# All eight depthwise chunks on VectorE instead of seven beside one on GpSimd, with value and gate products in turn

## The chip, the core and the metric

The kernel runs on one core of a Trainium2 chip. The metric is the device time of one execution in microseconds, here the median of three runs. Lower is better.

## The reference

The kernel computes one step of a diffusion trunk of two layers, for 512 latent tokens and 128 context tokens of 1024 features, all float32. The first layer mixes tokens by a Conformer convolution, the second by a bidirectional Mamba-2 scan; each is followed by an expert-choice mixture of 16 experts. This case is about the convolution of the first layer:

```
def conformer_conv(h, pw1_w, pw1_b, dw_w, dw_b, ln_g, ln_b, pw2_w, pw2_b, axis):
    u = h @ pw1_w + pw1_b
    a, g = jnp.split(u, 2, axis=-1)
    u = a * jax.nn.sigmoid(g)
    ...
    v = depthwise_conv2d(grid, dw_w, dw_b, kh, kw).reshape(bsz, L, dm)
    v = jax.nn.silu(layer_norm(v, ln_g, ln_b))
    return v @ pw2_w + pw2_b
```

The pointwise product makes 2048 features of 1024. Its first half is the value, its second the gate. The depthwise convolution has 31 taps; the latent tokens are a grid of rows of 64, the context tokens one line of 128. Around it stand the modulation vectors, six per layer, from SiLU(cond) @ ada_w[i] + ada_b[i].

## The kernel before, in words

Five engines run programs written out by hand, tied by semaphores. Features lie on the 128 partitions, so the 1024 features are eight chunks (0 to 7), and a chunk holds 640 tokens.

SP only loads weights: units of 2 MB, in the order in which TensorE uses them, into a ring of three slots (`load`, L366 in it). Before a unit goes into a slot it waits until the unit three places earlier has been used; `used` says on which semaphore. Units 0 to 11 are the modulation of layer 0, 12 to 15 the pointwise product (value of chunks 0 to 3, gate of 0 to 3, value of 4 to 7, gate of 4 to 7), 16 to 27 the modulation of layer 1, 28 and 29 the second pointwise product.

TensorE makes the modulation of layer 0 and the transposed input, then the 16 chunk products of the pointwise layer (L469, L470; 512 and 128 tokens), two in flight. It makes them in the order of the units: value of chunks 0 to 3, gate of 0 to 3, and then the same for 4 to 7. Then comes the modulation of layer 1 (L407, L398), and only then the mean over the features of the convolved chunks (L480, L481: a product with a matrix of 1/1024), one chunk after the other in a fixed order, each as soon as its chunk is convolved, and the mean of the squares (L485, L486). Then the second pointwise product.

ScalarE empties the banks. Of a value chunk it writes three pieces into the padded rows `upad` (L917, L919, L921); of a gate chunk it writes sigmoids into `sig` (L924, L926). Each such chunk raises `glu_a` by one.

VectorE and GpSimd share the convolution. `glu` (L313, L315, L318) multiplies value and sigmoid in place. Then a chunk has one product (L1324) and 30 multiply-adds, called taps here (L1328, SCALAR_TENSOR_TENSOR on 128 x 640), into the chunk of `v`. VectorE takes seven chunks in the groups (0), (1, 2), (4, 5), (6, 7):

```
step.sync(len(chunks) - 1 - (j if k == TAPS - 1 else 0))
ins = V.scalar_tensor_tensor(out, rows(k), dw_w[:, c, k:k + 1], out, ALU.mult, ALU.add)
```

`sync(n)` waits until all steps but the last n are complete. In a pair the taps of its two chunks stand in turn and each waits for the last but one; in the lone chunk 0 each waits for the one before. GpSimd takes chunk 3: a product into a buffer (L1162) and an addition (L1164) for each tap. When all eight chunks and their mean are there, VectorE centres them (L1338, L1340), ScalarE squares, TensorE sums, and VectorE goes on to the reciprocal and the scaling (L1342 to L1349).

Of the kernel before, what the change touches and what calls it, by code (L numbers as in the profile page):

```python
# [19 lines left out]
ALU = mybir.AluOpType  # L20
# [3 lines left out]
P = 128  # L24
# [31 lines left out]

CONV_DVE = ((0,), (1, 2), (4, 5), (6, 7))
CONV_ORDER = [c for cs in CONV_DVE for c in cs]
CONV_POOL = (3,)

# [54 lines left out]
def build(nc, w_stream, x_in, params, consts, router, w_dt, ln_rows, pw2_b, ssd_rows, state_in, y_out, state_out):  # L115
    ctx = ExitStack()
    with ctx:
# [56 lines left out]
        sig = take("conv", KC, TOK)  # L174
        pconv = take("conv", 2, TOK)
        sq = take("conv", 2, TOK)
# [88 lines left out]
        def par_v(name, *shape):  # L265
# [13 lines left out]
        landed = [sem(f"slot_landed{i}") for i in range(R)]  # L279
        names = """wo_high wo_low yT_low lgT_ready logits_tr pool_step glu_sig_pool conv_pool x_loaded par_loaded cst_loaded wr_loaded ln_loaded pwb_loaded ssdp_loaded state_loaded  # L280
            dve_step act_step adab_ready cond_ready ada_mm mrow_ready ada_tr mT_ready
# [27 lines left out]
        def glu(c, eng, step, gated, n_gated):  # L309

            i = (c // 4) * 8 + 4 + c % 4
            step.eng.wait_ge(s["glu_a"], i + 1)
            step(eng.tensor_tensor(upad[:, c, 0:8, HALO:HALO + GRID_W], upad[:, c, 0:8, HALO:HALO + GRID_W],  # L313
                                   sig[:, c, 0:SAMPLE].rearrange("p (r w) -> p r w", w=GRID_W), ALU.mult))
            step(eng.tensor_tensor(upad[:, c, 8, HALO:PITCH], upad[:, c, 8, HALO:PITCH],  # L315
                                   sig[:, c, SAMPLE:SAMPLE + PITCH - HALO], ALU.mult))
            step.sync()
            eng.tensor_tensor(upad[:, c, 9, 0:PITCH - HALO], upad[:, c, 9, 0:PITCH - HALO],  # L318
                              sig[:, c, SAMPLE + GRID_W - HALO:TOK], ALU.mult).then_inc(gated, 1)
            step.eng.wait_ge(gated, n_gated)  # L320
# [7 lines left out]
        def _(sp):  # L328
# [7 lines left out]
            def used(u):  # L336
# [3 lines left out]
                if u < U_ADA1:  # L340
                    return s["pw1_done"], 4 * (u - U_PW1 + 1)
                if u < U_PW2:
# [44 lines left out]
        def _(pe):  # L387
# [74 lines left out]
            for i in range(16):  # L462
                if i % 4 == 0:
                    w = unit_wait(U_PW1, i // 4)
                if i >= 2:
                    pe.wait_ge(s["glu_a"], i - 1)
                for k in range(KC):
                    lw = w[:, k, (i % 4) * P:(i % 4 + 1) * P]
                    pe.matmul(bank[i % 2][:, :], lw, hT[:, k, 0:SAMPLE], start=(k == 0), stop=(k == KC - 1))  # L469
                    ins = pe.matmul(bank[2 + i % 2][:, 0:P], lw, hT[:, k, SAMPLE:TOK], start=(k == 0), stop=(k == KC - 1))  # L470
# [3 lines left out]
            pe.wait_ge(s["glu_a"], 16)  # L474
            for i, k in enumerate(CONV_ORDER[:5] + list(CONV_POOL) + CONV_ORDER[5:]):
                if k in CONV_ORDER:
                    pe.wait_ge(s["conv_ready"], CONV_ORDER.index(k) + 1)
                else:
                    pe.wait_ge(s["conv_pool"], CONV_POOL.index(k) + 1)
                pe.matmul(bank[0][:, :], mean_w, v[:, k, 0:SAMPLE], start=(i == 0), stop=(i == KC - 1))  # L480
                ins = pe.matmul(bank[2][:, 0:P], mean_w, v[:, k, SAMPLE:TOK], start=(i == 0), stop=(i == KC - 1))  # L481
            ins.then_inc(s["mean_mm"], 1)
# [372 lines left out]
        def _(act):  # L855
# [55 lines left out]
            for i in range(16):  # L911
                c = (i // 8) * 4 + i % 4
                act.wait_ge(s["pw1_done"], i + 1)
                a, b = bank[i % 2], bank[2 + i % 2]
                if (i // 4) % 2 == 0:
                    bias = pw1_b[:, c:c + 1]
# [223 lines left out]
        def _(pool):  # L1140
# [14 lines left out]
            pool_step = Steps(pool, s["pool_step"])  # L1155
            for c in CONV_POOL:
                glu(c, nc.gpsimd, pool_step, s["glu_sig_pool"], CONV_POOL.index(c) + 1)
                out, rows = taps(c)
                pool_step(nc.gpsimd.tensor_scalar(out, rows(0), dw_w[:, c, 0:1], dw_b[:, c:c + 1], ALU.mult, ALU.add))
                for k in range(1, TAPS):  # L1160
                    prod = pconv[:, k % 2, :].rearrange("p (r w) -> p r w", w=GRID_W)
                    pool_step(nc.gpsimd.tensor_scalar(prod, rows(k), dw_w[:, c, k:k + 1], None, ALU.mult))  # L1162
                    pool_step.sync()
                    ins = nc.gpsimd.tensor_tensor(out, out, prod, ALU.add)  # L1164
                    if k < TAPS - 1:
                        pool_step(ins)
                    else:
                        ins.then_inc(s["conv_pool"], 1)

            def ln_shift(b):  # L1170
# [86 lines left out]
        def _(dve):  # L1257
# [58 lines left out]

            for chunks in CONV_DVE:
                for c in chunks:
                    glu(c, V, step, s["glu_sig"], CONV_ORDER.index(c) + 1)
                for k in range(TAPS):  # L1320
# [12 lines left out]

            dve.wait_ge(s["conv_ready"], len(CONV_ORDER))
            dve.wait_ge(s["conv_pool"], len(CONV_POOL))
            dve.wait_ge(s["mean_mm"], 1)
# [471 lines left out]
```

## Time and profile before

| | before |
|---|---|
| median of three runs | 3122.15 us (3120.74 to 3125.72) |
| profiled execution | its span, 3126.8 us, is the one time on record for it |
| TensorE busy | 2657.5 us, 85% of the span |
| VectorE busy | 2156.3 us, 69% |
| ScalarE busy | 1293.1 us, 41% |
| GpSimd busy | 736.0 us, 24% |

The shares are over the whole span; this case turns on the stretch from about 100 to 425 us. Matmuls of float32 appear as two records each. The times of the section with rows count from the start of the span. GpSimd's durations are rough.

### The profile page before, as it was taken

Reading aid. Unit: us, or ns where it says so; the run is one execution under the profiler, and the core shown is the slowest. Engines: PE = TensorE matmul, PEld = TensorE weight load, DVE = VectorE, ACT = ScalarE, POOL = GpSimd, SP = SyncE. Lnnn points to the kernel's source line nnn. Section 1 sums busy time; section 2 is a strip of 40 time slices with the busy share of each in tenths; the row PEclk is TensorE's granted clock in tenths of the full one; section 3 lists DMA queues with packets and bytes.
Section 4 is the critical chain, followed back from the end, with each engine's and each line's share of the span. In section 5 each row is a group of like instructions: output and inputs, shape, how many; then the busy total and the mean of one; then the engine's idle time right before and its main releaser. Section 6 shows DMA issues by size and latency. Waiting matters only on the chain. (4 is left out here: it accounts for less than half of the span.)

```text
span 3126.8 us, 31580 instructions
## 1 busy us (share of the span) xinstructions
PE 2657.5 (85%) x11808; PEld 1683.5 (54%) x11808; DVE 2156.3 (69%) x2454; ACT 1293.1 (41%) x1573; POOL 736.0 (24%) x345
## 2 busy tenths in 40 slices
PE   8999377888989888939989899898578889988892
PEld 1452133566656666526756556565356665666661
DVE  0099934777786777774656747567777778777777
ACT  1211022556566565622212212122255657656562
POOL 1069002121221212230422304133312121121213
PEclk9999788899999999968999999999789999999996
DMA  8316201566676666721011010110146667666770
GB/s 354 135 54 241 108 3 65 197 257 244 243 296 241 256 244 252 282 73 36 12 68 41 34 69 6 68 54 34 41 182 253 243 263 292 237 250 242 266 269 34
DMA packets 37578, 511.06 MB, mean 163 GB/s; under 512 B 4336, under 2 KB 4352, under 8 KB 6384
## 3 DMA queue, kind: packets, MB, share of 16 engines
q1 hardware_dynamic: 35424, 500.96, 42.8%
q0 software_dynamic: 2064, 8.87, 0.8%
q8 instruction: 60, 0.98, 0.1%
q14 instruction: 30, 0.25, 0.0%
HBM read 505.10 MB, written 4.72 MB: 163 GB/s over the span
## 5 line engine op out<-in xcount | busy, mean ns | idle before, releaser
L970 ACT ACTIVATE w_h<-ring 128x2048 fp32r<-128x2048 f32 x384 | 731.4, 1914 | 277.5 <-PE bank L564 266.9
L1407 DVE TENSOR_TENSOR w_l<-ring,w_h 128x2048 fp32r<-128x2048 f32 x320 | 736.9, 2320 | 132.0 <-ACT w_h L970 131.6
L1148 POOL TENSOR_TENSOR w_l<-ring,w_h 128x2048 fp32r<-128x2048 f32 x64 | 291.8, 4581 | 1331.9 <-ACT w_h L970 1331.9
L562 PE MATMUL bank<-w_h,xin_h 128*80 128x512 f32 x1024 | 409.6, 400 | 35.5 <-DVE w_l L1407 25.8
L563 PE MATMUL bank<-w_l,xin_h 128*80 128x512 f32 x1024 | 403.2, 394 | 0.0
L564 PE MATMUL bank<-w_h,xin_l 128*80 128x512 f32 x1024 | 401.2, 392 | 0.0
L562 PEld LDWEIGHTS bank<-w_h,xin_h 128*80 128x80 f32 x1024 | 151.8, 148 | 144.9 <-DVE w_l L1407 60.3
L1328 DVE SCALAR_TENSOR_TENSOR scr<-scr,par 128x640 f32<-128x640 f32 x210 | 221.4, 1120 | 1.1
L562 PE MATMUL bank<-w_h,hidT_h 128*80 128x512 f32 x512 | 204.7, 400 | 10.1 <-DVE hidT_l L1399 9.1
L563 PE MATMUL bank<-w_l,hidT_h 128*80 128x512 f32 x512 | 202.5, 396 | 0.0
L564 PE MATMUL bank<-w_h,hidT_l 128*80 128x512 f32 x512 | 201.0, 393 | 0.0
L671 PE MATMUL bank<-hT,ring 128*128 128x512 f32 x384 | 198.9, 600 | 2.3 <-DVE scr L1722 2.3
L564 PEld LDWEIGHTS bank<-w_h,xin_l 128*80 128x80 f32 x1024 | 152.1, 149 | 85.3 <-issue 0.9
L563 PEld LDWEIGHTS bank<-w_l,xin_h 128*80 128x80 f32 x1024 | 152.0, 148 | 73.4 <-issue 0.7
L407 PE MATMUL bank<-ring,csil 128*2 128x512 f32 x384 | 169.8, 596 | 10.8 <-DMA ring<-w_stream 10.8
L1226 POOL TENSOR_TENSOR scr<-cst,scr 128x512 f32<-128x512 f32 x80 | 97.9, 1248 | 335.5 <-ACT scr L1075 271.0
L515 PE MATMUL bank<-scr,X 128*128 128x128 f32 x1024 | 152.5, 323 | 0.0
L1398 DVE CAST hidT_h<-bank 128x320 fp32r<-128x320 f32 x64 | 31.1, 485 | 174.0 <-PE bank L570 174.0
L515 PEld LDWEIGHTS bank<-scr,X 128*128 128x128 f32 x1024 | 150.5, 239 | 0.0
L692 PE MATMUL bank<-ring,hT 128*128 128x512 f32 x320 | 149.7, 594 | 0.0
L508 PE MATMUL bank<-scr,X 128*128 128x32 f32 x256 | 57.9, 402 | 101.4 <-DVE scr L1381 101.4
L469 PE MATMUL bank<-hT,ring 128*128 128x512 f32 x256 | 131.0, 594 | 0.0
(260 smaller groups left out, 4286.5 us busy)
## 6 DMA issues: line engine op xcount, KB each, us to landing
ring<-w_stream SPq DMA_DIRECT2D x234, 2048.0 KB, 7.8
ln_gb<-ln_rows POOLq DMA_DIRECT2D x4, 1024.0 KB, 5.1
ring<-w_stream SPq DMA_DIRECT2D x4, 1024.0 KB, 5.0
X<-x_in SPq DMA_DIRECT2D x1, 2560.0 KB, 25.7
y_out<-X SPq DMA_DIRECT2D x5, 512.0 KB, 2.6
scr<-state_in POOLq DMA_DIRECT2D x8, 256.0 KB, 7.3
state_out<-scr POOLq DMA_DIRECT2D x8, 256.0 KB, 5.0
cst<-consts SPq DMA_DIRECT2D x1, 480.0 KB, 11.5
```

The costliest lines, as they stand in the source:

```text
L407: ins = pe.matmul(bank[4 + u % 2][0:2, :], csil[:, k, :], w[:, k, :], start=(k == 0), stop=(k == KC - 1))
L469: pe.matmul(bank[i % 2][:, :], lw, hT[:, k, 0:SAMPLE], start=(k == 0), stop=(k == KC - 1))
L515: ins = pe.matmul(bank[6 + half][:, kk * P:(kk + 1) * P], X[:, t, k * P:(k + 1) * P], psel[:, t, :, :], start=(t == 0), stop=(t == NS - 1))
L562: pe.matmul(out[0:SLOTS, :], ah[:, c, :], wh[:, k, :], start=(c == 0), stop=False)
L563: pe.matmul(out[0:SLOTS, :], ah[:, c, :], wl[:, k, :], start=False, stop=False)
L564: ins = pe.matmul(out[0:SLOTS, :], al[:, c, :], wh[:, k, :], start=False, stop=(c == KC - 1))
L671: pe.matmul(bank[i % 2][:, :], w[:, k, c0:c0 + P], hT[:, k, 0:SAMPLE], start=(k == 0), stop=(k == KC - 1))
L692: ins = pe.matmul(bank[(0, 6, 7, 0, 1)[t]][:, :], hT[:, k, t * P:(t + 1) * P], w[:, k, :], start=(k == 0), stop=(k == KC - 1))
L970: A(w_h[m % NB][:, :, :], src, ACT.Copy).then_inc(s["high_ready"], 1)
L1148: nc.gpsimd.tensor_tensor(w_l[m % NB][:, :, :], src, w_h[m % NB][:, :, :].bitcast(F32), ALU.subtract).then_inc(s["low_pool"], 1)
L1328: ins = V.scalar_tensor_tensor(out, rows(k), dw_w[:, c, k:k + 1], out, ALU.mult, ALU.add)
L1407: V.tensor_tensor(w_l[m % NB][:, :, :], src, w_h[m % NB][:, :, :].bitcast(F32), ALU.subtract)\
```

## The change

Four things are changed.

- GpSimd convolves nothing; chunk 3 goes to VectorE, whose groups are now (0), (1), (2, 3), (4, 5), (6, 7).
- TensorE makes value and gate of a chunk in turn, so chunk 0 has both after two products. ScalarE empties them in that order. The order of the weight units is as before, so that two units are in use at a time, and SP waits for other counts: `(7, 8, 15, 16)` chunk products instead of `(4, 8, 12, 16)`.
- The lone chunks 0 and 1 are summed in two halves, taps 0 to 15 into `v` and taps 16 to 30 into `pconv`, which stand in turn; one addition joins them.
- TensorE takes the means in the order of the chunks.

```
-CONV_DVE = ((0,), (1, 2), (4, 5), (6, 7))
-CONV_ORDER = [c for cs in CONV_DVE for c in cs]
-CONV_POOL = (3,)
+CONV_GROUPS = ((0,), (1,), (2, 3), (4, 5), (6, 7))
+SPLIT_TAP = 16
...
-            i = (c // 4) * 8 + 4 + c % 4
-            step.eng.wait_ge(s["glu_a"], i + 1)
+            step.eng.wait_ge(s["glu_a"], 2 * c + 2)
...
-                    return s["pw1_done"], 4 * (u - U_PW1 + 1)
+                    return s["pw1_done"], (7, 8, 15, 16)[u - U_PW1]
...
             for i in range(16):
-                if i % 4 == 0:
-                    w = unit_wait(U_PW1, i // 4)
+                c, half = i // 2, i % 2
+                w = unit_wait(U_PW1, 2 * (c // 4) + half)
                 if i >= 2:
                     pe.wait_ge(s["glu_a"], i - 1)
                 for k in range(KC):
-                    lw = w[:, k, (i % 4) * P:(i % 4 + 1) * P]
+                    lw = w[:, k, (c % 4) * P:(c % 4 + 1) * P]
...
-            for i, k in enumerate(CONV_ORDER[:5] + list(CONV_POOL) + CONV_ORDER[5:]):
-                if k in CONV_ORDER:
-                    pe.wait_ge(s["conv_ready"], CONV_ORDER.index(k) + 1)
-                else:
-                    pe.wait_ge(s["conv_pool"], CONV_POOL.index(k) + 1)
...
+            for k in range(KC):
+                pe.wait_ge(s["conv_ready"], k + 1)
...
-                c = (i // 8) * 4 + i % 4
+                c = i // 2
...
-                if (i // 4) % 2 == 0:
+                if i % 2 == 0:
...
-            for c in CONV_POOL:
-                glu(c, nc.gpsimd, pool_step, s["glu_sig_pool"], CONV_POOL.index(c) + 1)
-                out, rows = taps(c)
-                pool_step(nc.gpsimd.tensor_scalar(out, rows(0), dw_w[:, c, 0:1], dw_b[:, c:c + 1], ALU.mult, ALU.add))
-                for k in range(1, TAPS):
-                    prod = pconv[:, k % 2, :].rearrange("p (r w) -> p r w", w=GRID_W)
-                    pool_step(nc.gpsimd.tensor_scalar(prod, rows(k), dw_w[:, c, k:k + 1], None, ALU.mult))
-                    pool_step.sync()
-                    ins = nc.gpsimd.tensor_tensor(out, out, prod, ALU.add)
...
+            def conv_alone(c):
+
+                glu(c, V, step, s["glu_sig"], c + 1)
+                out, rows = taps(c)
+                half = pconv.rearrange("p (r w) -> p r w", w=GRID_W)
+                step(V.tensor_scalar(out, rows(0), dw_w[:, c, 0:1], dw_b[:, c:c + 1], ALU.mult, ALU.add))
+                step(V.tensor_scalar(half, rows(SPLIT_TAP), dw_w[:, c, SPLIT_TAP:SPLIT_TAP + 1], None, ALU.mult))
+                for k in range(1, SPLIT_TAP):
+                    step.sync(1)
+                    step(V.scalar_tensor_tensor(out, rows(k), dw_w[:, c, k:k + 1], out, ALU.mult, ALU.add))
+                    if SPLIT_TAP + k < TAPS:
+                        step.sync(1)
+                        step(V.scalar_tensor_tensor(half, rows(SPLIT_TAP + k), dw_w[:, c, SPLIT_TAP + k:SPLIT_TAP + k + 1],
+                                                    half, ALU.mult, ALU.add))
+                step.sync()
+                V.tensor_tensor(out, out, half, ALU.add).then_inc(s["conv_ready"], 1)
+                dve.wait_ge(s["conv_ready"], c + 1)
```

How the order of instructions moves can be seen at two places. The first is ScalarE where it begins to empty the pointwise product; `upad` and `sig` are both parts of the scratch tile `scr`. Before, the fourth value chunk is followed by the first sigmoid:

```order
L917 ACTIVATE scr<-bank,par 128x8x64 [waits pw1_done]
L919 ACTIVATE scr<-bank,par 128x79
L921 ACTIVATE scr<-bank,par 128x79 [waits act_step]
L924 ACT_TABLE_LOAD
L924 ACTIVATE scr<-bank,par 128x512 [waits pw1_done]
```

Of the change, where the lines have moved up by five, from the first value chunk on:

```order
L912 ACTIVATE scr<-bank,par 128x8x64 [waits pw1_done,upad_zero]
L914 ACTIVATE scr<-bank,par 128x79
L916 ACTIVATE scr<-bank,par 128x79 [waits act_step]
L919 ACT_TABLE_LOAD
L919 ACTIVATE scr<-bank,par 128x512 [waits pw1_done]
L921 ACTIVATE scr<-bank,par 128x128 [waits act_step]
L912 ACTIVATE scr<-bank,par 128x8x64 [waits pw1_done]
```

The first sigmoid stood behind four value chunks and now stands behind one. The other sigmoids and value chunks follow in turn.

The second place is VectorE at chunk 0, from its gating to the gating of the next chunk. Before:

```order
L313 TENSOR_TENSOR scr<-scr 128x8x64 [waits glu_a]
L315 TENSOR_TENSOR scr<-scr 128x79
L318 TENSOR_TENSOR scr<-scr 128x79 [waits dve_step]
L1324 TENSOR_SCALAR scr<-scr,par 128x640 [waits glu_sig]
L1328 SCALAR_TENSOR_TENSOR scr<-scr,par 128x640 [waits dve_step] x30
```

Of the change, whose L1325 adds to `v` and L1328 to `pconv`; between the pieces the two stand in turn, 29 in all:

```order
L1321 TENSOR_SCALAR scr<-scr,par 128x640 [waits glu_sig]
L1322 TENSOR_SCALAR scr<-scr,par 128x640
L1325 SCALAR_TENSOR_TENSOR scr<-scr,par 128x640 [waits dve_step]
L1328 SCALAR_TENSOR_TENSOR scr<-scr,par 128x640 [waits dve_step]
...
L1325 SCALAR_TENSOR_TENSOR scr<-scr,par 128x640 [waits dve_step]
L1331 TENSOR_TENSOR scr<-scr 128x640 [waits dve_step]
L311 TENSOR_TENSOR scr<-scr 128x8x64 [waits glu_a,conv_ready]
```

Thirty taps behind each other have become 29 in two chains, with a second product ahead and a sum behind.

## Rows read from the trace of the kernel before

**Rows 1.** The first line of the page

```profile
span 3126.8 us, 31580 instructions
```

**Rows 2.** Busy time of each engine by stretch, granted clock and DMAs

```profile
core 0: us, PE busy (x) PEld busy (x) DVE busy (x) ACT busy (x) POOL busy (x), PEclk, DMA share, GB/s
...
181.00:311.00 130.00, 130.00 (x418) 51.07 (x417) 129.61 (x103) 17.90 (x56) 127.31 (x64) 1.00 0.46 170
311.00:337.00 26.00, 25.57 (x75) 6.06 (x74) 26.00 (x32) 5.04 (x23) 0.82 (x1) 1.00 0.79 283
337.00:393.00 56.00, 7.04 (x25) 3.97 (x24) 55.70 (x75) 0.32 (x3) 0.00 (x0) 0.59 0.08 34
393.00:412.00 19.00, 16.07 (x40) 8.14 (x38) 8.27 (x19) 7.18 (x9) 0.00 (x0) 0.68 0.00 0
```

**Rows 3.** Timeline of VectorE, the convolution: start, us, line, operation, count

```profile
154.63 0.69 DVE L313 TENSOR_TENSOR scr<-scr 128x512 f32<-128x512 f32 x1 [47.55 <-ACT scr L926]
...
156.44 28.39 DVE L1328 SCALAR_TENSOR_TENSOR scr<-scr,par 128x640 f32<-128x640 f32 x30
...
190.24 84.38 DVE L1328 SCALAR_TENSOR_TENSOR scr<-scr,par 128x640 f32<-128x640 f32 x60
...
341.87 0.68 DVE L313 TENSOR_TENSOR scr<-scr 128x512 f32<-128x512 f32 x1
...
344.33 1.14 DVE L1324 TENSOR_SCALAR scr<-scr,par 128x640 f32<-128x640 f32 x2
345.38 47.83 DVE L1328 SCALAR_TENSOR_TENSOR scr<-scr,par 128x640 f32<-128x640 f32 x60
```

**Rows 4.** Taps (L1328) alone in two stretches: us, VectorE busy (count), clock, DMA

```profile
159.20:175.77 16.57, 15.93 (x18) 1.00 0.00 0
...
312.00:341.00 29.00, 29.00 (x37) 1.00 0.78 284
```

**Rows 5.** Timeline of GpSimd, one tap of chunk 3 to the next

```profile
252.84 2.46 POOL L1162 TENSOR_SCALAR scr<-scr,par 128x640 f32<-128x640 f32 x1
...
257.06 2.45 POOL L1162 TENSOR_SCALAR scr<-scr,par 128x640 f32<-128x640 f32 x1
```

**Rows 6.** Timeline of ScalarE, the second, fifth and eighth product emptied

```profile
127.55 0.69 ACT L917 ACTIVATE scr<-bank,par 128x512 f32<-128x512 f32 x1 [7.33 <-PE bank L470]
...
153.51 0.69 ACT L924 ACTIVATE scr<-bank,par 128x512 f32<-128x512 f32 x1 [6.08 <-PE bank L470]
...
179.47 0.69 ACT L924 ACTIVATE scr<-bank,par 128x512 f32<-128x512 f32 x1 [7.57 <-PE bank L470]
```

**Rows 7.** Timeline of TensorE, the means of the chunks

```profile
336.49 1.12 PE L480 MATMUL bank<-scr,cst 128*128 128x512 f32 x2
...
337.67 1.02 PE L480 MATMUL bank<-scr,cst 128*128 128x512 f32 x2
...
338.75 1.02 PE L480 MATMUL bank<-scr,cst 128*128 128x512 f32 x2
...
392.47 2.07 PE L480 MATMUL bank<-scr,cst 128*128 128x512 f32 x2 [47.76 <-DVE scr L1328]
```

**Rows 8.** Timeline of VectorE, centring, after the variance, and scaling

```profile
397.24 0.69 DVE L1338 TENSOR_TENSOR scr<-scr,bank 128x512 f32<-128x512 f32 x1 [4.03 <-PE bank L481]
...
411.08 0.69 DVE L1342 TENSOR_SCALAR scr<-bank 128x512 f32<-128x512 f32 x1 [6.39 <-PE bank L486]
...
416.97 5.97 DVE L1349 TENSOR_TENSOR scr<-scr 128x640 f32<-128x640 f32 x8 [0.80 <-ACT scr L934]
```

**Rows 9.** Timeline of TensorE, the means of the squares

```profile
399.07 2.07 PE L485 MATMUL bank<-scr,cst 128*128 128x512 f32 x2 [1.97 <-ACT scr L932]
...
405.33 1.02 PE L485 MATMUL bank<-scr,cst 128*128 128x512 f32 x2
...
409.80 1.02 PE L485 MATMUL bank<-scr,cst 128*128 128x512 f32 x2
```

**Rows 10.** DMA issues of the page: count, KB each, us from issue to landing

```profile
ring<-w_stream SPq DMA_DIRECT2D x234, 2048.0 KB, 7.8
```

More of the change, by code:

```diff
@@ L174, in build @@
         sig = take("conv", KC, TOK)
-        pconv = take("conv", 2, TOK)
+        pconv = take("conv", TOK)
         sq = take("conv", 2, TOK)
@@ L279, in build @@
         landed = [sem(f"slot_landed{i}") for i in range(R)]
-        names = """wo_high wo_low yT_low lgT_ready logits_tr pool_step glu_sig_pool conv_pool x_loaded par_loaded cst_loaded wr_loaded ln_loaded pwb_loaded ssdp_loaded state_loaded
+        names = """wo_high wo_low yT_low lgT_ready logits_tr pool_step x_loaded par_loaded cst_loaded wr_loaded ln_loaded pwb_loaded ssdp_loaded state_loaded
             dve_step act_step adab_ready cond_ready ada_mm mrow_ready ada_tr mT_ready
@@ L474, in _ @@
             pe.wait_ge(s["glu_a"], 16)
-            for i, k in enumerate(CONV_ORDER[:5] + list(CONV_POOL) + CONV_ORDER[5:]):
-                if k in CONV_ORDER:
-                    pe.wait_ge(s["conv_ready"], CONV_ORDER.index(k) + 1)
-                else:
-                    pe.wait_ge(s["conv_pool"], CONV_POOL.index(k) + 1)
-                pe.matmul(bank[0][:, :], mean_w, v[:, k, 0:SAMPLE], start=(i == 0), stop=(i == KC - 1))
-                ins = pe.matmul(bank[2][:, 0:P], mean_w, v[:, k, SAMPLE:TOK], start=(i == 0), stop=(i == KC - 1))
+            for k in range(KC):
+                pe.wait_ge(s["conv_ready"], k + 1)
+                pe.matmul(bank[0][:, :], mean_w, v[:, k, 0:SAMPLE], start=(k == 0), stop=(k == KC - 1))
+                ins = pe.matmul(bank[2][:, 0:P], mean_w, v[:, k, SAMPLE:TOK], start=(k == 0), stop=(k == KC - 1))
             ins.then_inc(s["mean_mm"], 1)
@@ L1155, in _ @@
             pool_step = Steps(pool, s["pool_step"])
-            for c in CONV_POOL:
-                glu(c, nc.gpsimd, pool_step, s["glu_sig_pool"], CONV_POOL.index(c) + 1)
-                out, rows = taps(c)
-                pool_step(nc.gpsimd.tensor_scalar(out, rows(0), dw_w[:, c, 0:1], dw_b[:, c:c + 1], ALU.mult, ALU.add))
-                for k in range(1, TAPS):
-                    prod = pconv[:, k % 2, :].rearrange("p (r w) -> p r w", w=GRID_W)
-                    pool_step(nc.gpsimd.tensor_scalar(prod, rows(k), dw_w[:, c, k:k + 1], None, ALU.mult))
-                    pool_step.sync()
-                    ins = nc.gpsimd.tensor_tensor(out, out, prod, ALU.add)
[L1165 to L1168, printed above, removed]
             def ln_shift(b):
@@ L1315, in _, with conv_group @@
             hT_evac(0)
-            for chunks in CONV_DVE:
+            def conv_group(chunks):
                 for c in chunks:
-                    glu(c, V, step, s["glu_sig"], CONV_ORDER.index(c) + 1)
+                    glu(c, V, step, s["glu_sig"], c + 1)
                 for k in range(TAPS):
@@ L1332, in _ @@
                             ins.then_inc(s["conv_ready"], 1)
-            dve.wait_ge(s["conv_ready"], len(CONV_ORDER))
-            dve.wait_ge(s["conv_pool"], len(CONV_POOL))
+            def conv_alone(c):
+                glu(c, V, step, s["glu_sig"], c + 1)
+                out, rows = taps(c)
[12 more added lines that the diff above has]
+                dve.wait_ge(s["conv_ready"], c + 1)
+            for chunks in CONV_GROUPS:
+                if len(chunks) == 1:
+                    conv_alone(chunks[0])
+                else:
+                    conv_group(chunks)
+            dve.wait_ge(s["conv_ready"], KC)
             dve.wait_ge(s["mean_mm"], 1)
```

## The prediction

> **What bounds the kernel now.** The execution spans 3126.8 us [rows 1]; the median of the runs shown is 3122.15, so the span lies 4.65 above it. The sum below is a difference between instants of this one execution, and it is taken off the median.
>
> I read the page's 40 slices first: the fifth (312 to 391 us) is where TensorE is emptiest while VectorE is full. The table by stretches [rows 2] makes that sharp. From 181 to 311 us TensorE, VectorE and GpSimd are all full. From 337 to 393 TensorE works 7.04 of 56 us, VectorE 55.70 and GpSimd nothing: TensorE waits 47.76 us for the last taps, and they end it at 392.47 [rows 7]. So the end of this stage is set by VectorE's chain of taps, which starts at 154.63 us, having waited 47.55 us for ScalarE's first sigmoid, and ends at 345.38 + 47.83 = 393.21 [rows 3].
>
> Two things in that chain are to be seen. First its start: ScalarE empties the product of the pointwise layer chunk by chunk, 8.65 us apart, and the sigmoid that starts at 153.51 is the fifth of the 16 [rows 6]. Second its pace. The sixty taps of chunks 1 and 2 take 84.38 us (1.406 each), those of chunks 6 and 7 take 47.83 (0.797 each) [rows 3]. The fast ones ran with GpSimd silent, the slow ones beside it; GpSimd makes one tap in 257.06 - 252.84 = 4.22 us [rows 5], and three slow VectorE taps are 4.22 us too. From 312 to 341 us, after GpSimd's last tap, 37 taps fit in 29 us (0.784), while the DMAs and TensorE run as hard as in the slow stretch [rows 2, 4]. That singles out GpSimd.
>
> **The change, part by part.**
>
> *GpSimd's chunk goes.* Chunk 3 moves to VectorE. No GpSimd work lies beside the taps any more, so I price every interleaved tap at 0.797. Later GpSimd work is not touched. Nothing waited on GpSimd here: its last tap was done by about 312 us, 80 before VectorE's.
>
> *Value and gate in turn.* TensorE's 16 chunk products have the same size and total, and ScalarE's evacuations only change order. The first gate is now the second product instead of the fifth: ScalarE gets it at 127.55, where it now empties a value chunk after 7.33 us of idling [rows 6], and VectorE may start 3 x 8.65 = 25.96 us sooner, at 154.63 - 25.96 = 128.67. The table load that now falls before this sigmoid comes in that idle time of ScalarE and costs nothing; in the old order too there is one only. The gate of chunk 1 is there 17.3 us later, at 146.0, and that of chunk 3 at about 180.6 (it is the eighth product before and after: ScalarE starts on it at 179.47 and takes 1.1 [rows 6]).
>
> *SP's queue.* Unit 15 of the weights (gates of chunks 4 to 7) waits for unit 12's slot, which is free after the seventh product instead of the fourth: 153.51 + 2 x 8.65 = 170.8 us, counted from the fifth. A transfer lands 7.8 us after issue [rows 10], so at 178.6; the tenth product begins when the ninth is out, at 188.1. Unit 17 now waits for the 15th product instead of the 12th (240.0 us), lands at 247.8 and is the second of the modulation's units, wanted some 7 us after that starts at about 248.6. The slack is 9 and 8 us; if it were gone, each us late would be TensorE's. Units 16 and 18 are freed as before.
>
> *Lone chunks in two half sums.* Chunks 0 and 1 each cost: gating and first product 156.44 - 154.63 = 1.81; one more product 1.14/2 = 0.57; 29 alternating taps; the final sum, which waits for everything: a 640-wide TENSOR_TENSOR is 0.75 [rows 8], and 0.25 for the two semaphore turns is an estimate from the 0.125 by which a lone tap's spacing exceeds an interleaved one's. The 29 taps are the term with two candidates. In the old lone chunk, where every tap waits for the one before, 18 taps take 16.57 us, 0.921 each [rows 4]; interleaved ones take 0.797 [rows 3]. The new order lets each tap wait for the last but one, as the pairs do, so I take 0.797: 23.1 us, and 26.5 for the chunk. The upper bound is 0.921: 3.6 us more a chunk, 7.2 in all. Lower bound 0.784: 0.4 less.
>
> The Trainium skill ("VectorE: DVE Perf Modes", section "The DRAIN you can't avoid") says that a semaphore between chained VectorE instructions costs nothing, since the pipeline empties anyway. By it the half sums would buy nothing and the lone chunk would take 0.921 a tap either way, with an extra product and sum on top; the rows at 0.921 and 0.797 speak against it.
>
> *Sum for VectorE.* 128.67 + 2 x 26.5 = 181.7, when chunk 3's gate is there. A pair without GpSimd takes 393.21 - 341.87 = 51.34 [rows 3]; three take 154.0. The taps end at **335.7 us**, against 393.21.
>
> *What is late next.* TensorE. It ends the second modulation at 336.5 and goes straight on to the means [rows 7]. The eight chunks' means now stand behind each other: the spacing is 338.75 - 337.67 = 1.08, the eighth starts at 337.67 + 6 x 1.08 = 344.15 and VectorE can have it 1.28 later, as behind the last variance matmul of the same two shapes (409.80 to 411.08 [rows 8, 9]). VectorE begins to centre at **345.4** instead of 397.24 [rows 8]: **51.8 us** gained. VectorE has slack: chunk 6 is wanted at 344.15 - 1.08 = 343.1, 7.4 after my end of the taps. So even at 0.921 a tap in the lone chunks (342.9) the sum hardly moves.
>
> *The clock.* From 337 to 393 the granted clock averages 0.59, from 393 to 412 0.68 [rows 2]: after its wait TensorE works at the lower of its levels (1.2 GHz) until about 404. The first three variance chunks now take (405.33 - 399.07)/3 = 2.09 us each, the late ones (409.80 - 405.33)/4 = 1.12 [rows 9]. In the new order TensorE arrives from full work at 2.4 GHz and idles about 2 us only. First variance matmul 1.83 us after centring begins, as now; eight at 1.12, the last 1.28: 1.83 + 7 x 1.12 + 1.28 = 10.95, against 411.08 - 397.24 = 13.84 [rows 8]. Gain **2.9 us**. Bounds: 0 if the clock falls in the short pause; for more than 2.9 no row speaks.
>
> Behind 411.08 the same work stands in the same order, each step waiting for the one before, and the ring of three weight slots is filled by TensorE's own progress, so nothing can be done ahead or given back there. Sum: 51.8 + 2.9 = 54.7; 3122.15 - 54.7 is about **3067.5 us** (-1.75%).
>
> **Rivals.**
>
> A. *Taps end after TensorE wants them* (chance 0.10). If lone taps take 0.921 or more, or paired taps beside ScalarE's evacuations over 0.83, chunk 6 is late and every further us is lost, and TensorE may drop a clock level once more. At 0.85 for all 238 taps VectorE ends at 348.3, 5.2 later than wanted, and with the clock's 2.9 lost the time is 3075.6. Against it: 29 us at 0.784 with both other engines at work [rows 4].
>
> B. *It is not GpSimd that slows the taps* (0.03), but some other companion of that stretch, ending at about 312 by chance. Then chunk 3 is simply added to a slow VectorE. Break-even: the 238 taps plus 17.3 us of other work must fit in 393.21 - 128.67 = 264.5, so they may take 1.04 each; above that it is **slower**. At 1.406 for all, the taps take 334.6, and the end comes 87 us later than now: 3209. What speaks for it: GpSimd's stretch is also that of the pointwise product [rows 2]. Against: chunk 4 and 5's own taps turn fast the moment GpSimd stops, under the same transfers at 283 GB/s [rows 2, 4].
>
> C. *The Trainium skill's lock* (0.02 as a result of its own). As a mechanism here: if in each 4.22 us GpSimd kept VectorE out only for part, and VectorE's spacing alone were still above 0.797 for other reasons, removing GpSimd would give less. Halfway, 1.1 a tap, VectorE would end at 408 and the kernel take 3137. The skill ("SBUF — State Buffer", section "Who interferes with whom") has it as an exclusive lock on a shared port pair, the loser waiting for a whole instruction. By that rule the removal frees all of it; the fast rows agree, but three VectorE taps for each pair of GpSimd instructions, which is busy 127.31 of 130 us [rows 2], are more than a strict reading would allow.
>
> D. *The early order does not arrive* (0.03): a weight unit late, or TensorE waiting for ScalarE in the mixed order, shifts the end of the modulation. A landing twice the usual 7.8 us would still be inside unit 15's slack; I price this at up to 6 us lost, 3073.
>
> **How the numbers follow.** Forecast, with TensorE the bound at 345.4: chance 0.82. Its own range is 3063 to 3073: the clock term between 0 and 2.9, half a us each in the start of the means and in the landing of the last one, and 3 us for the spread of medians (the three runs shown lie 5 apart). To hold 8 in 10 with room for A and D I give 3060 to 3076. A measurement of this kernel tells about 0.2% (6 us) from no change. Faster by more than that: forecast, A, D: 0.95. Slower by more: B and part of C, 0.04. Within: 0.01.
>
> **What would show it.** VectorE's first gating near 128.7 us and its last tap near 335.7; the spacing of taps 0.80 from first to last, the lone chunks' as well, about 26.5 us for each of those; no wait of TensorE for taps at all, the eight means behind each other from 336.5; centring from 345.4, variance done by about 356.4, TensorE's clock full until then; everything later moved by 54 to 55 us and of equal length. Wrong it is if the taps keep 1.0 or more, if TensorE idles before the sixth or seventh mean, or if the pointwise product ends later than 248.6.

## The result and the profile after

| | before | after |
|---|---|---|
| median (range, runs) | 3121.44 us (3119.01 to 3125.72, 4) | 3072.82 us (3066.08 to 3075.05, 4) |
| ratio, 95% interval | | 0.983, 0.9814 to 0.9847 |
| profiled execution: time, span | span 3126.8 us | 3066.08, 3064.2 us |
| VectorE's last tap ends | 393.21 us | 334.58 us |
| centring starts | 397.24 us | 345.61 us |
| first residual after the second product | 435.16 us | 380.17 us |

The kernel is 1.7% faster: the medians differ by 48.6 us. The interval of the ratio stands for a gain of 48 to 58 us, and the forecast of 54.7 lies in it. The profiled execution happens to be the fastest of the four.

The stretches of [rows 2], of the changed kernel, with the same columns:

```profile
core 0: us, PE busy (x) PEld busy (x) DVE busy (x) ACT busy (x) POOL busy (x), PEclk, DMA share, GB/s
...
181.00:311.00 130.00, 130.00 (x419) 51.14 (x418) 129.55 (x176) 17.91 (x56) 0.00 (x0) 1.00 0.47 170
311.00:337.00 26.00, 25.57 (x76) 6.06 (x74) 23.58 (x30) 4.95 (x23) 0.00 (x0) 1.00 0.78 282
337.00:393.00 56.00, 40.20 (x112) 19.09 (x111) 20.95 (x32) 17.49 (x23) 0.00 (x0) 0.88 0.08 34
393.00:412.00 19.00, 19.00 (x44) 7.49 (x42) 2.77 (x4) 0.00 (x0) 0.00 (x0) 1.00 0.00 1
```

From 181 to 311 us VectorE is as busy as before, and so is TensorE, at the same DMA load; but VectorE completes 176 instructions instead of 103. Busy time alone would have told nothing here: before, VectorE was counted as busy while it was held up inside its instructions. From 337 to 393 us TensorE was idle for 56 - 7.04 = 49 us before and is for 56 - 40.20 = 16 us now, 13.86 of them in one wait behind the variance. Most of the low clock went with it: the granted clock of this stretch rose from 0.59 to 0.88.

VectorE's timeline, beside [rows 3] and [rows 8]:

```profile
128.76 0.69 DVE L311 TENSOR_TENSOR scr<-scr 128x512 f32<-128x512 f32 x1 [21.59 <-ACT scr L921]
...
154.10 0.82 DVE L1331 TENSOR_TENSOR scr<-scr 128x640 f32<-128x640 f32 x1
154.97 0.69 DVE L311 TENSOR_TENSOR scr<-scr 128x512 f32<-128x512 f32 x1
...
184.53 47.84 DVE L1310 SCALAR_TENSOR_TENSOR scr<-scr,par 128x640 f32<-128x640 f32 x60
...
286.75 47.83 DVE L1310 SCALAR_TENSOR_TENSOR scr<-scr,par 128x640 f32<-128x640 f32 x60
345.61 0.69 DVE L1343 TENSOR_TENSOR scr<-scr,bank 128x512 f32<-128x512 f32 x1 [11.03 <-PE bank L476]
...
356.60 0.69 DVE L1347 TENSOR_SCALAR scr<-bank 128x512 f32<-128x512 f32 x1 [3.55 <-PE bank L481]
```

The chain starts at 128.76 (forecast 128.67). A lone chunk takes 154.97 - 128.76 = 26.2 us (26.5). Sixty taps beside the pointwise product take 47.84 us, as long as the sixty that now end the chain. And the wait has changed sides: VectorE waits 11.03 us for TensorE's means, where TensorE waited 47.76 for VectorE.

TensorE's timeline, beside [rows 7] and [rows 9]:

```profile
336.58 1.13 PE L475 MATMUL bank<-scr,cst 128*128 128x512 f32 x2
...
344.26 1.02 PE L475 MATMUL bank<-scr,cst 128*128 128x512 f32 x2
...
347.44 1.12 PE L480 MATMUL bank<-scr,cst 128*128 128x512 f32 x2 [1.94 <-ACT scr L927]
...
355.32 1.02 PE L480 MATMUL bank<-scr,cst 128*128 128x512 f32 x2
```

Eight means run back to back, the eighth from 344.26; the clock holds over the pause of 1.94 us, and the last variance chunk starts 7.88 us after the first, seven spacings of 1.13.

### The profile page after: what moved, and what is told of

It reads as the page before. It is cut to its first block and busy times, and to the rows that moved or that the text cites. A ratio compares the mean times of both kernels' runs of the same rounds, so it can differ in the third digit from the quotient of the medians.

```text
span 3064.2 us, 31565 instructions
## 1 busy us (share of the span) xinstructions
PE 2645.6 (86%) x11808; PEld 1675.3 (55%) x11808; DVE 2123.2 (69%) x2490; ACT 1293.3 (42%) x1573; POOL 607.1 (20%) x281
## 5 line engine op out<-in xcount | busy, mean ns | idle before, releaser
L666 PE MATMUL bank<-hT,ring 128*128 128x512 f32 x384 | 196.9, 594 | 2.3 <-DVE scr L1727 2.3
L1157 POOL TENSOR_TENSOR X<-X,ln_gb 128x1024 f32<-128x1024 f32 x16 | 39.1, 2441 | 552.9 <-ACT X L896 552.9
L1310 DVE SCALAR_TENSOR_TENSOR scr<-scr,par 128x640 f32<-128x640 f32 x180 | 143.5, 876 | 0.0
```

The lines of the kernel that those rows point to most:

```text
L666: pe.matmul(bank[i % 2][:, :], w[:, k, c0:c0 + P], hT[:, k, 0:SAMPLE], start=(k == 0), stop=(k == KC - 1))
```

## The experiments

### The two halves of the change apart

First only the order of the products, in the kernel before; GpSimd keeps chunk 3:

```
-                c = (i // 8) * 4 + i % 4
+                c = i // 2
...
-                if (i // 4) % 2 == 0:
+                if i % 2 == 0:
```

with the same edit on TensorE, in SP's counts and in `glu`.

> The kernel before with value and gate products in turn alone; GpSimd keeps chunk 3, the groups of VectorE and the whole sum of chunk 0 stay. Theory (GpSimd's stream slows the taps beside it to 1.4 us, only the interplay counts): VectorE gates chunk 0 at 128.7 and is through with it at about 158; it then waits until about 163.3 for the gate of chunk 2; GpSimd works from 180.6 to about 312 as before; the last tap ends near 373 instead of 393.2, so the time falls by about 20 us. Rival (the taps are slow for another reason, tied to the pointwise product): the slow stretch begins when VectorE starts, and the last tap comes later than 380. No change at all would mean that the start of VectorE's chain is not what counts.

Measured: 3101.86 us, ratio 0.9941 (0.9922 to 0.996). VectorE's taps of the three pairs:

```profile
165.84 47.84 DVE L1327 SCALAR_TENSOR_TENSOR scr<-scr,par 128x640 f32<-128x640 f32 x60
...
218.83 83.84 DVE L1327 SCALAR_TENSOR_TENSOR scr<-scr,par 128x640 f32<-128x640 f32 x60
...
308.22 63.72 DVE L1327 SCALAR_TENSOR_TENSOR scr<-scr,par 128x640 f32<-128x640 f32 x60
```

and GpSimd's timeline where it begins:

```profile
180.92 34.55 POOL L312 TENSOR_TENSOR scr<-scr 128x512 f32<-128x512 f32 x1 [171.46 <-ACT scr L925]
215.43 0.32 POOL L314 TENSOR_TENSOR scr<-scr 128x79 f32<-128x79 f32 x1
```

The time fell by 18.9 us, for an expected 20, and the end of the taps came as expected, 308.22 + 63.72 = 371.94 against 373, but not by the expected way. GpSimd did not slow the pair that was under way when it started: it stood still for 34.55 us, until the pair's last tap (165.84 + 47.84 = 213.68) and VectorE's next gating, and VectorE kept 0.797 a tap. Only then were both slow, and GpSimd's chunk was done at 344.2 instead of the expected 312. In the kernel before GpSimd got in at once: its first instruction, at 180.64, took 1.66 us. VectorE was then at the lone chunk 0, whose taps, 0.92 apart and 0.876 long, leave a gap between them. So my picture of a slow-down beside GpSimd was incomplete: it matters who is in first. That the gap is what let GpSimd in is a reading of this one case; no run changes the gap alone.

Then the other half alone, the changed kernel with the old order of the products (the edit above reversed):

> The changed kernel with the order of the products set back to that of before (values of four chunks, then their gates). Theory: VectorE starts at 154.6 as before, all its taps take 0.797, and it needs the same 205.8 us as in the changed kernel, so the last tap ends at 360.4; centring starts at about 364 instead of 397.2, some 33 us gained against before, with TensorE at 1.2 GHz for the last means. Rival (it is not GpSimd that slows the taps): taps stay at 1.3 to 1.4 beside the pointwise product and the end is later than 400.

Measured: 3093.68 us, ratio 0.9916 (0.9899 to 0.9934). VectorE's timeline:

```profile
154.53 0.69 DVE L312 TENSOR_TENSOR scr<-scr 128x512 f32<-128x512 f32 x1 [47.55 <-ACT scr L922]
...
312.53 47.84 DVE L1311 SCALAR_TENSOR_TENSOR scr<-scr,par 128x640 f32<-128x640 f32 x60
364.36 0.69 DVE L1344 TENSOR_TENSOR scr<-scr,bank 128x512 f32<-128x512 f32 x1 [3.99 <-PE bank L477]
```

The last tap ends at 360.37 (expected 360.4) and all of them are fast. Rival B is out: beside the same matmuls and transfers the taps are fast once GpSimd is silent, and one more chunk on VectorE ends 32.8 us sooner than one chunk fewer. This half also holds the half sums of chunks 0 and 1, which the next run prices at 6.3 us of the last tap; the larger part, some 26 us, is GpSimd's. Centring moves by 32.9 us with this half and by 21.3 with the other (375.97 in its trace), 54.2 together, against 51.6 with both: TensorE takes over as the bound before the second half has had its whole effect. The median moved by 27.1 us only, less than the 33 of centring; in its profile the lead over the second profile of the kernel before shrinks from 34.1 us behind the second product to 30.7 at the end, a loss that the profiles of other kernels share (see below).

### The half sums

```
             for chunks in CONV_GROUPS:
-                if len(chunks) == 1:
-                    conv_alone(chunks[0])
-                else:
-                    conv_group(chunks)
+                conv_group(chunks)
```

> The changed kernel with chunks 0 and 1 as one sum each, every tap waiting for the one before. Theory of the prediction: these taps take 0.92 instead of 0.797, each of the two chunks some 3.3 us longer, the last tap ends at about 341.1 instead of 334.6, TensorE still waits for nothing and centring starts at 345.6 as in the changed kernel: same time within the spread. Rival (the half sums buy time): centring comes 6 us later. Rival (a wait between chained VectorE instructions costs nothing): taps of these chunks at 0.80 and the last tap no later than 334.6.

Measured: 3072.21 us, ratio 0.9839 (0.9823 to 0.9855), the changed kernel's own time. VectorE:

```profile
130.68 27.59 DVE L1310 SCALAR_TENSOR_TENSOR scr<-scr,par 128x640 f32<-128x640 f32 x30
...
293.08 47.83 DVE L1310 SCALAR_TENSOR_TENSOR scr<-scr,par 128x640 f32<-128x640 f32 x60
345.72 0.69 DVE L1340 TENSOR_TENSOR scr<-scr,bank 128x512 f32<-128x512 f32 x1 [4.81 <-PE bank L476]
```

27.59 us for 30 taps is 0.92 each; the last tap ends at 340.91 instead of 334.58, 6.3 us later, and centring starts where it did, since VectorE only waits less (4.81 instead of 11.03 us). The half sums work and buy nothing here. The first residual came at 381.81 instead of 380.17, since the first tile of the second product took 10.11 us at a low clock. The rule of the Trainium skill that was weighed in the prediction ("VectorE: DVE Perf Modes", "The DRAIN you can't avoid"), that the semaphore between chained instructions costs nothing, does not hold for these: both forms wait on a semaphore, and the wait for the instruction just before costs 0.12 us a tap more than the wait for the last but one.

### What GpSimd does to VectorE

Three kernels give GpSimd a stream of work that nobody needs, into a scratch tile, in the changed kernel; ScalarE waits for its end before its squares. They differ in the instruction, in its number (50, 50 and 100) and in the start; this is the first:

```
+            pool.wait_ge(s["cst_loaded"], 16)
+            pool.wait_ge(s["glu_a"], 8)
+            for k in range(50):
+                pool_step.sync(1 if k else 0)
+                pool_step(nc.gpsimd.tensor_tensor(sq[:, k % 2, :], cst[:, 0:TOK], cst[:, 256:256 + TOK], ALU.add))
```

> The changed kernel, and GpSimd busy with work nobody needs: from the eighth emptied chunk on (180.6 us, VectorE between two groups) 50 TENSOR_TENSOR additions on 128 x 640, two inputs in SBUF. Theory (the two engines exclude each other where both read SBUF, and whoever has the way keeps it while its instructions overlap): GpSimd gets in at the gap between chunk 1 and the pair, and the pair's taps slow to 1.3 to 1.7 us while the stream lasts. Rival (it was the alternation of two kinds of instruction or the shared chunk of the padded rows that cost): taps stay at 0.80.

```profile
194.38 101.60 DVE L1319 SCALAR_TENSOR_TENSOR scr<-scr,par 128x640 f32<-128x640 f32 x60
```

From 195 to 280 us, first the taps alone, then GpSimd's additions alone (us, busy time and count, clock, DMA):

```profile
195.00:280.00 85.00, 85.00 (x42) 1.00 0.36 130
```

```profile
195.00:280.00 85.00, 85.00 (x42) 1.00 0.36 130
```

42 taps and 42 additions: turns, one for one, 2.02 us for the two, slower than the 1.3 to 1.7 that I had expected. The one execution took 3133.66 us, above all nine of the kernel before that were timed with it (3119.22 to 3130.89): the taps end at 398.21, later than before. The rival, that only the mix of instructions or the shared rows of the input cost, is out.

The second has one input instead of two, `tensor_scalar(sq[:, k % 2, :], cst[:, 0:TOK], 2.0, None, ALU.mult)`, and starts one chunk later, with VectorE in the middle of a pair:

> The same with 50 TENSOR_SCALAR products, one input, started from the ninth emptied chunk (about 189 us), when VectorE is in the middle of the taps of chunks 2 and 3. Theory (VectorE's overlapped taps keep GpSimd out until a gap; seen in the run with the order alone, where GpSimd's first instruction took 34.55 us and ended where the pair did): the first GpSimd instruction spans from 189 to about 233, the taps of chunks 2 and 3 stay at 0.797, and from 233 on taps and products hold each other up. Rival (they share by turns from the start): the first instruction takes about 2 us and the taps slow at once at 189.

```profile
189.63 45.14 POOL L1156 TENSOR_SCALAR scr<-cst 128x640 f32<-128x640 f32 x1 [180.17 <-issue]
```

```profile
184.50 47.84 DVE L1319 SCALAR_TENSOR_TENSOR scr<-scr,par 128x640 f32<-128x640 f32 x60
...
236.28 61.58 DVE L1319 SCALAR_TENSOR_TENSOR scr<-scr,par 128x640 f32<-128x640 f32 x60
```

As expected: the product that started at 189.63 stood for 45.14 us, to 234.77, while the pair under way lost nothing. Afterwards, from 237 to 296 us, taps and GpSimd's products:

```profile
237.00:296.00 59.00, 59.00 (x59) 1.00 0.74 268
```

```profile
237.00:296.00 59.00, 59.00 (x29) 1.00 0.74 268
```

Two taps for each product. Now the kernel before can be read: a GpSimd tap there is one product and one addition [rows 5], in which VectorE gets two taps and one. Its own trace has it so, in timelines of single instructions of VectorE and GpSimd behind the product that starts at 252.84:

```profile
253.46 1.42 DVE L1328 SCALAR_TENSOR_TENSOR scr<-scr,par 128x640 f32<-128x640 f32 x1
...
254.81 0.87 DVE L1328 SCALAR_TENSOR_TENSOR scr<-scr,par 128x640 f32<-128x640 f32 x1
...
255.38 1.69 POOL L1164 TENSOR_TENSOR scr<-scr 128x640 f32<-128x640 f32 x1
...
255.61 2.15 DVE L1328 SCALAR_TENSOR_TENSOR scr<-scr,par 128x640 f32<-128x640 f32 x1
```

Two taps start beside the product, and the one that starts beside the addition takes 2.15 us instead of 0.88. That gives the three taps in 4.22 us on which the prediction had stumbled. The one execution took 3084.36 us.

The third only writes, 100 memsets of the same tile:

> The same with 100 memsets of 128 x 640, which write SBUF and read nothing. Theory (only reads collide, VectorE's second input against GpSimd's input): the taps keep 0.797 and the last one ends at 334.6 as in the changed kernel. Rival (any GpSimd access holds VectorE up): taps at 1.1 or more beside the stream.

GpSimd, and VectorE beside it:

```profile
180.71 57.45 POOL L1156 MEMSET scr<- 128x640 f32 x100 [171.24 <-issue]
```

```profile
183.42 55.60 DVE L1315 TENSOR_SCALAR scr<-scr,par 128x640 f32<-128x640 f32 x2
238.94 1.67 DVE L1319 SCALAR_TENSOR_TENSOR scr<-scr,par 128x640 f32<-128x640 f32 x2
```

Neither theory had this. The chunks' first products, TENSOR_SCALARs, took 55.60 us where they take 1.14: with one memset every 0.57 us, VectorE was not through with them until the last memset was done. The gating TENSOR_TENSORs just before, at 182.26, took their usual time beside the same memsets. So no tap ever ran beside a memset: the taps kept 0.797 behind them and the last one ended at 388.98, not at the expected 334.6, and whether taps and memsets collide stays open. Why the one-input TENSOR_SCALAR was held and the two-input TENSOR_TENSOR was not, no run here tells. The one execution took 3117.61 us.

### Is TensorE the bound now?

If TensorE's work ahead of the means sets the time in the changed kernel, then less of it there must pay. The modulation of layer 1 is not needed before layer 1, and TensorE idles 13.9 us behind the variance. So the last two of its twelve units go there (the last one in a further kernel), with TensorE's small transposes and ScalarE's evacuation of them behind the first tiles of the second pointwise product:

```
-            ada(1, U_ADA1)
+            tr = ada(1, U_ADA1, 12 - LATE)
...
+            for u in range(12 - LATE, 12):
+                w = unit_wait(U_ADA1, u)
+                pe.wait_ge(s["mrow_ready"], 12 + u - 1)
+                for k in range(KC):
+                    ins = pe.matmul(bank[4 + u % 2][0:2, :], csil[:, k, :], w[:, k, :],
+                                    start=(k == 0), stop=(k == KC - 1))
+                ins.then_inc(s["ada_mm"], 1)
             pe.wait_ge(s["v_ready"], 8)
```

> The changed kernel with the last two of the twelve modulation units of layer 1 taken out from ahead of the means and put behind the variance, where TensorE idles 13.9 us before the second pointwise product. Theory (TensorE ahead of the means is what bounds the changed kernel there, 11 us behind VectorE's last tap): TensorE is through with ten units and six means by about 329, waits 5 us for the taps, centring starts at about 336.5 instead of 345.6, the two units (14 us) fill the gap and keep the clock up, so the second product starts about when ScalarE is done, with its first tile at 7.1 instead of 9.1 us: 9 to 11 us faster than the changed kernel, about 3062. Rival (the clock falls in the new pause of 5 us): 2 to 4 us of it are lost in the variance. Rival (that stretch is not critical): same time.

Measured: 3061.22 us, ratio 0.9799 (0.9781 to 0.9816). TensorE's timeline:

```profile
333.80 2.07 PE L477 MATMUL bank<-scr,cst 128*128 128x512 f32 x2 [5.09 <-DVE scr L1326]
...
350.35 13.89 PE L489 MATMUL bank<-ring,csil 128*2 128x512 f32 x32
364.28 7.13 PE L507 MATMUL bank<-ring,scr 128*128 128x512 f32 x16
```

Both parts are there: a pause of 5.09 us before the last two means, with the clock down behind it (2.07 us for the first), and the two units fill the gap exactly, so that the first tile takes 7.13 instead of 8.59 us. Centring came at 337.83, 1.3 later than expected, because of the clock, and the variance took 12.62 us instead of 10.99: the rival of the clock came true in part, beside the theory. The first residual is at 372.57, 7.6 us before that of the changed kernel.

Then one unit late and two, timed together with the changed kernel:

> The changed kernel again, timed beside the next two. The gain against before should be 54 to 55 us where all stages are alike, so a ratio near 0.9825, with single runs up to 5 us off either way by where TensorE's clock falls.

> One modulation unit instead of two behind the variance. Theory: eleven units and eight means keep TensorE busy without a pause until 338, centring starts at 338.3 with the clock up, the variance takes 10.95 and is done at 349.3, the unit takes 7 of the 13.9 us of idling behind it; the second product starts at about 363.2. If the clock is still up there, its first tile takes 7.1, and VectorE's first residual comes at 371.5; if it has fallen 2 us later. So within 1 us of the kernel with two units late, and some 8 us faster than the changed kernel. Rival (nothing is won, as the stretch is not critical): same time as the changed kernel.

> Two units late, timed on the same chip as the changed kernel. By its first trace VectorE's first residual comes 7.6 us earlier than in the changed kernel (372.57 instead of 380.17); the rest is equal work, so the medians should be 6 to 10 us apart. Rival (the later stages eat it up by their clock): medians less than 3 us apart.

| | median (range), us | ratio to before, interval |
|---|---|---|
| the changed kernel | 3074.79 (3068.07 to 3075.27) | 0.9834, 0.9819 to 0.9849 |
| one unit late | 3060.25 (3058.56 to 3066.03) | 0.9795, 0.9781 to 0.981 |
| two units late | 3061.75 (3058.72 to 3067.83) | 0.9802, 0.9785 to 0.9819 |

The changed kernel gained 49.2 us on the kernel before this time, again some 5 less than expected. With one unit late the means end without a pause (centring at 338.28, expected 338.3) and the variance is done at 349.28 (349.3), but the clock falls once more in the 6.91 us that stay empty:

```profile
349.17 7.03 PE L489 MATMUL bank<-ring,csil 128*2 128x512 f32 x16
363.11 8.70 PE L507 MATMUL bank<-ring,scr 128*128 128x512 f32 x16 [6.91 <-ACT scr L947]
```

Either is faster than the changed kernel, by 14.5 and 13.0 us on the medians, and the ranges do not meet. For two units 6 to 10 us had been expected. The traces account for 7.7 and 7.5 us up to the first residual (372.96 and 373.16, for 380.64 in the changed kernel of the same timing), so TensorE's work ahead of the means was the bound. The rest is not shown to belong to the change: of the profiled executions, the one with one late unit leads the changed kernel's by 8.3 us at 1500 us and by 8.1 at the end, the one with two by 5.9 and by 12.2, and that growth comes behind 1500 us, where the next section finds losses that come and go. Between one and two late units nothing can be told.

### The profiles against each other

The profiled execution gained 62.6 us of span (3126.8 to 3064.2), 8 more than the stages up to the second product. The place was found by laying ScalarE's instructions of the two traces side by side: the distance is 55 to 57 us from 490 to 1350 and 62 to 64 from 1440 on. Two more profiles were taken for it, one of each kernel:

> The kernel before once more, for its profile. In its first profile TensorE's clock is low for 17 us from 1415 on, at the first matmuls of the scan layer; no profile of the other kernels has that stretch. Theory (a chance of that execution): it is missing here, and the span lies 54 to 56 us above that of the changed kernel's profiles instead of 62.6. Rival (it belongs to the kernel before): it is there again.

> The changed kernel once more, for its profile. The four runs lie 9 us apart, and the profiled one gained 62.6 us of span where the stages up to the second pointwise product account for 55. Theory (the granted clock falls in some executions and not in others in the first matmuls of the scan layer): up to 1340 us this trace agrees with the first one within 2 us, and differences arise where low-clock stretches differ, above all just behind the long idle stretch of TensorE around 1300 to 1350. Rival (the change itself shortens the scan layer): the stretch from 1300 to 1450 has the same length and clock as in the first profile.

The changed kernel's second profile did not settle it. The distance between its two profiles is 1.2 us at 1350 (3 us for a moment about 1000), and from 1344 to 1378 us the clock is 0.90 where the first has 0.92, in a stretch of the same length. By the terms set beforehand that spoke for the rival, that the change itself shortens the scan layer; it is the second profile of the kernel before that decides. The kernel before in its first and in its second profile, at the first matmuls of the scan layer (columns as in [rows 2]):

```profile
1415.00:1433.00 18.00, 18.00 (x73) 15.48 (x73) 3.77 (x9) 2.22 (x3) 0.00 (x0) 0.53 0.00 1
```

```profile
1415.00:1433.00 18.00, 18.00 (x102) 12.98 (x102) 9.00 (x18) 3.10 (x5) 0.00 (x0) 1.00 0.01 1
```

The same 18 us at clock 0.53 and at 1.00. The second profile spans 3119.8 us, and its distance from the first grows from 0.3 to 8.5 us there, of which 6.8 stay. So these were a chance of the execution whose rows the prediction used, and not an effect of the change. The three profiles of the changed kernel span 3064.2, 3069.0 and 3072.1 us at mean clocks of 0.927, 0.926 and 0.925. The distances from the second profile of the kernel before are thus 48 to 56 us; 54 to 56 had been expected, and only the first lies there. With ScalarE's instructions laid beside those of that profile, all three are 54.4 to 55.6 us ahead at 1500 (the times of this comparison are that profile's). The first keeps this to the end. The second loses 3.2 us between 1500 and 1700, where its clock is lower (0.97 instead of 1.00 from 1600 to 1700 of its own time). The third is still 54.5 ahead at 1900, 48.7 at 2100 and 47.6 at 2375: most of it is lost in the last part of the scan layer. A loss of 3 to 4 us between 1500 and 1700 also stands in the profiles of both halves, of the whole sums and of the late units, and in neither profile of the kernel before. Whether the changed kernel meets such losses more often than the kernel before is open; three profiles against two do not tell.

## Why the prediction was right

- **Where the bound was.** Right. VectorE's chain set the end of the stage and its start waited for ScalarE's first sigmoid: each half of the change alone moved the last tap, by 21.3 and 32.8 us. Both together moved it by 58.6, 4.5 more than the sum; with the order alone VectorE had waited 4.26 us for the gate of chunk 2, a wait that the changed kernel does not have.
- **The earlier start**: 25.96 us forecast, 25.87 in the trace. SP's changed counts cost nothing: TensorE has no wait for a weight unit between 100 and 440 us.
- **The pace of the taps**: 0.797 throughout, in the lone chunks too. (The 0.784 that the prediction took for a lower bound was no pace of its own: 37 taps in 29 us counts those that the window cuts, and they too stand 0.796 apart.) Last tap forecast 335.7, measured 334.58; the lone chunks were 0.3 us shorter each and the pairs 51.1 instead of 51.34.
- **TensorE late next**: 345.4 forecast, 345.61 measured, with a gain of 51.6 for 51.8. That VectorE had slack was shown by the whole sums, which used 6.3 us of it for nothing.
- **The clock term**: 2.9 forecast; the variance takes 10.99 instead of 13.84 us, 2.85 gained. The first tile of the second product varies by half a us with the place where the clock rises, 9.10 before and 8.59 after. The first residual came 54.99 us earlier, for a forecast of 54.7.
- **The median** is 5.3 us above the forecast, inside the range, and the gain 48.6 us instead of 54.7. The term that fails is the last: "the same work stands in the same order" is true of the work, but not of its time. Against the second profile of the kernel before, the three of the changed kernel have 54.4 to 55.6 us of gain at 1500 and 47.7 to 55.6 at the end, since the granted clock differs from one execution to the next, and I had taken a difference of two single instants for one of medians. That the first timing fell inside my inner range, 3063 to 3073, is partly luck: 3072.82 just does, and the second timing's 3074.79 does not.
- **Rival A** (taps late) did not come: nothing was slower than 0.797, and 7.4 us of slack were 8.6. **Rival B** is refuted by the run with the old order. **Rival D**: both weight units were in time.
- **Rival C** and the sentence beside it were where I was wrong about the mechanism. I held three taps for a pair of GpSimd instructions against the rule of the Trainium skill ("SBUF — State Buffer", "Who interferes with whom": an exclusive lock on a shared pair of ports, where the loser waits for a whole instruction). The streams show the strict reading to be nearer than I gave it credit for: one tap to one addition, two to one product. They also show what it does not say: the loser can be held not for one instruction but for a whole chain of them, 34.55, 45.14 and 55.60 us.

## What to carry to other kernels

Taking work off a full VectorE and giving it to GpSimd can cost VectorE more than the work: here one chunk of eight on GpSimd made VectorE's taps beside it 1.41 us instead of 0.80, and seven chunks beside GpSimd took 238.6 us from the first gating to the last tap, eight alone 205.8 (212.0 with whole sums). The busy share doesn't show this; compare the duration, or better the spacing, of the same instruction with and without the other engine. Once the longest chain has been cut, look at which engine waits now: here it was TensorE, and moving work that nobody waits for into its next idle stretch paid again, 7.5 us in the traces. And a gain read from one profile of each kernel carries the chance of both: here one low stretch of the clock in one of them was worth 6 of 62.6 us.

## What the hardware did that was not expected

- VectorE's taps, each waiting only for the last but one, overlap (0.876 us long, 0.797 apart), and in both cases where a GpSimd instruction that reads SBUF started beside them it did not get in before they ended: 34.55 and 45.14 us for instructions that take about 2.
- The other way round a chain of GpSimd memsets, 0.57 us apart, kept two VectorE TENSOR_SCALARs waiting for 55 us, but not the TENSOR_TENSORs just before them.
- Once GpSimd is in, the two take turns: 42 taps to 42 two-input additions, 59 taps to 29 one-input products.
- TensorE's granted clock was 0.53 on the mean of 18 us of unbroken matmuls in one execution (1.2 GHz for all but about one of them) and 1.00, 2.4 GHz, in the next execution profiled; that alone was worth some 6 us.
